# One attention loop in place of two, keys first in the context projection, and three experts over all tokens

## The chip, the cores and the metric

The kernel runs on one core of a Trainium2 chip. The metric is the device time of one execution in microseconds (us), the median of the runs. Everything is fp32 data; the large matrix products are made of three matmuls on `fp32r` halves (high by high, high by low, low by high), so that each weight tile is first split by ScalarE (ACT, `whi`) and VectorE (DVE, `wlo`) before TensorE (PE) uses it.

## The reference, cut to what matters

Two transformer blocks of two layers each over 256 tokens and 1024 channels. The change lies in layer two ("odd") of the first block: a projection, two attentions, an output projection, and a mixture of experts.

```python
p_lat = h_lat @ w_in                       # 256 x 2304: cq, dq, ck, cv, dk, dv
cq_l, dq_l = query_side(p_lat[..., :OD_Q], True)      # rms_norm by head, then rope
ck_l, cv_l, dk_l, dv_l = kv_side(p_lat[..., OD_Q:], True)
p_ctx = h_ctx @ w_in[:, OD_Q:]             # 256 x 1280: ck, cv, dk, dv of the context
ck_c, cv_c, dk_c, dv_c = kv_side(p_ctx, False)        # rms_norm and gain, no rope
y_lat = merge(window_gqa(cq_l, ck_l, cv_l, ck_c, cv_c, sink),      # 8 heads, sink in the sum
              diff_attention_latent(dq_l, dk_l, dv_l, dk_c, dv_c, lam))  # 4 heads, p0 - lam * p1
# merge: rms_norm over each difference head, concatenate, @ w_out

logits = xt @ router                       # 8 experts, the best 2 of each token
gates = ...                                # 256 x 8, zero where an expert was not chosen
out = sum over e of gates[:, e:e+1] * ((silu(xt @ w1[e]) * (xt @ w3[e])) @ w2[e])   # width 1408
```

## The kernel before, in words

**The weight stream.** SyncE (SP) loads weights in units of 512 rows by 512 columns (1 MB) into a ring of four buffers `raw`. ACT copies each half of a unit to `whi` (L326), DVE subtracts to `wlo` (L330), and PE runs the matmuls of L422, L423 and L426: 24 of them for a unit over both token tiles (`t` = 0, 1). `Split.step` on ACT and DVE splits the unit that comes two later; work between the halves of a step waits until PE has used the unit (`w_used`). A hook (`with_`) runs after each step with its number `i`: the small work of a stage is put there (`odd_q_*`, `odd_k_*`). Each engine runs its instructions in the order in which its function was written; semaphores join the engines. Nothing else decides the order.

**The projection of layer two.** `project_pe` makes the latent projection `pl` (blocks of 512 columns in the order of `OD_ORDER[0]`) and then the context projection `pc` (1280 columns: blocks of 512, 512 and 256). The first 128 columns of `pc` are the window keys, 128 are window values, then 512 difference keys and 512 difference values. During the context projection DVE finishes the latent keys: `odd_products_dve` and `odd_turn_dve` (rope, in hooks 1 and 2), `odd_scaled_dve` and `odd_twins_dve` with the root from GpSimd (POOL, `root_pool`), the lambda (hook 2), and then sums, gains and roots of the context keys (hooks 4 and 5). ACT waits in hook 4 for the sums `ss_c`. PE then transposes keys in `odd_k_pe` into `kTo`, first of all `out_done` and `k_lat`.

**The two attentions.** `attn_pe`, `attn_act` and `attn_dve` run a software pipeline over items: 16 window items (8 heads by 2 token tiles; scores of 512 keys and a mask matmul), then, as a second loop, 16 difference items. For item `i`, PE makes the scores of `i + 1`, transposes the probabilities of `i`, and makes the outputs of `i - 1`; DVE takes the maximum of the scores and copies the transposed probabilities of `i - 1` out of PSUM; ACT takes the exponential. Between the loops `heads_out_dve`, `heads_out_pe` and `heads_out_act` divide and transpose the window outputs. After the second loop `diff_out_dve` makes the difference, its squares and the root (POOL), scales, and PE transposes (`heads_out_pe(e, "att_d")`) between the two halves of the output projection `odd_out_pe`. All but the last of this chain lies on DVE alone.

**The experts.** `router_pe` and `router_dve` rank the logits, count the tokens of each expert and sort the experts by that count (`order`, `ids`); SP reads `ids` and loads the weights in that order. `wide(i)` is 2 for the first three experts of the order (256 slots) and 1 for the other five (128 slots). Tokens go into slots by a 0/1 matrix `sel`: `gather_pe` multiplies the rows of `x` (kept as `xmhi`, `xmlo`) by it, 16 matmuls a half, `select_pe` transposes it and picks the gates (`share`), and `scatter_pe` brings the outputs (`ohi`, `olo`) back to tokens. For the first three experts `added_dve` adds the scattered sum to `y`; from the fourth on the sums stay in PSUM.

## Time and profile before

| | |
|---|---|
| time, median of 3 runs | 2864.03 us (2858.02 to 2865.65) |
| the profiled execution: time / span | 2857.71 us / 2855.9 us |
| PE busy / weight loads | 2702.7 us (95%) / 2245.4 us |
| DVE, ACT, POOL busy | 1853.0 us (65%), 1466.5 us (51%), 164.1 us (6%) |
| chain that ended last, by engine | PE 84%, DVE 8%, ACT 3%, DMA 2%, issue 2% |
| HBM read | 507.33 MB, 178 GB/s over the span |

The profiled execution is 6.3 us under the median of the three runs. The chain is followed back from the last instruction: at each step to what released it, or to the instruction before it on its engine. A row of the timeline has its start, its length, the engine, the line of the kernel and, in brackets, how long the engine stood idle before it and what released it; consecutive instructions of one kind are merged, and their count follows the `x`. "PEclk" is TensorE's granted clock, with 1.00 for 2.4 GHz and 0.50 for 1.2 GHz.

### The profile page before, as it was taken

How to read it: one execution, taken by the hardware profiler on the slowest of the kernel's cores; microseconds unless marked ns; L12 is line 12 of the kernel's file. 1: busy time of each engine (PE TensorE's matmuls, PEld its weight loads, DVE VectorE, ACT ScalarE, POOL GpSimd, SP SyncE). 2: the span in 40 equal slices, each digit the busy share in tenths (PEclk: the TensorE clock that was granted, in tenths of full speed). 3: DMA queues.
4: the chain of work that ended last, by engine and by line, in shares of the span. 5: the costliest groups of instructions: out<-in, count | busy, mean ns of one | idle time of the engine just before them, and what ended most of it. 6: DMA issues, size and time to landing. Idle time of an engine off the chain costs nothing.

```text
span 2855.9 us, 34338 instructions
## 1 busy us (share of the span) xinstructions
PE 2702.7 (95%) x13129; PEld 2245.4 (79%) x13129; DVE 1853.0 (65%) x2344; ACT 1466.5 (51%) x2095; POOL 164.1 (6%) x206
## 2 busy tenths in 40 slices
PE   7998899999989889999999899998799999998998
PEld 5776678888875678888888788877678788787787
DVE  6676687787694555556878655588556555546555
ACT  6563454444462244445777545664355544563553
POOL 2111000000120000000000000002010000100100
PEclk9999999999998989999999999999899999999999
DMA  8672176776740045546999656540255555550444
GB/s 297 231 255 88 66 244 229 241 274 209 228 156 1 1 163 184 171 162 213 332 322 320 234 162 206 163 162 1 82 183 182 182 189 175 200 192 16 143 159 147
DMA packets 260641, 511.43 MB, mean 179 GB/s; under 512 B 9641, under 2 KB 40577, under 8 KB 260368
## 3 DMA queue, kind: packets, MB, share of 16 engines
q1 hardware_dynamic: 256576, 498.11, 51.7%
q0 software_dynamic: 3920, 11.36, 1.4%
q8 instruction: 95, 1.56, 0.2%
q14 instruction: 50, 0.41, 0.0%
HBM read 507.33 MB, written 1.05 MB: 178 GB/s over the span
## 4 chain that ended last, share of the span: by engine, by line
PE 84%; DVE 8%; ACT 3%; DMA 2%; issue 2%; POOL 0%; SPq 0%; DVEq 0%; ACTq 0%; POOLq 0%
PE bank L422 23%; PE bank L423 22%; PE bank L426 22%; PE bank L1378 2%; PE bank L1391 2%; DVE wlo L330 2%; DVE h_hid L2643 1%; PE bank L1404 1%; DMA raw<-in_moe_w 1%; PE bank L393 1%; PE bank L394 1%; PE bank L395 1%; ACT whi L326 1%; PE bank L2189 1%; PE bank L518 1%
## 5 line engine op out<-in xcount | busy, mean ns | idle before, releaser
L330 DVE TENSOR_TENSOR wlo<-raw,whi 128x1024 fp32r<-128x1024 f32 (+1 forms) x964 | 1140.8, 1199 | 693.8 <-ACT whi L326 687.8
L326 ACT ACTIVATE whi<-raw 128x1024 fp32r<-128x1024 f32 (+1 forms) x964 | 990.4, 1039 | 795.6 <-PE bank L426 757.7
L422 PE MATMUL bank<-whi,xhi 128*128 128x512 f32 (+2 forms) x2328 | 887.0, 381 | 20.1 <-DVE wlo L330 7.7
L426 PE MATMUL bank<-whi,xlo 128*128 128x512 f32 (+2 forms) x2328 | 878.2, 377 | 0.0
L423 PE MATMUL bank<-wlo,xhi 128*128 128x512 f32 (+2 forms) x2328 | 877.2, 377 | 0.0
L422 PEld LDWEIGHTS bank<-whi,xhi 128*128 128x128 f32 x2328 | 441.4, 190 | 102.1 <-issue 16.1
L426 PEld LDWEIGHTS bank<-whi,xlo 128*128 128x128 f32 x2328 | 440.5, 189 | 77.4
L423 PEld LDWEIGHTS bank<-wlo,xhi 128*128 128x128 f32 x2328 | 441.5, 190 | 74.6
L422 PE MATMUL bank<-whi,f_hhi 128*128 128x512 f32 x496 | 194.1, 391 | 0.0
L426 PE MATMUL bank<-whi,f_hlo 128*128 128x512 f32 x496 | 193.1, 389 | 0.0
L423 PE MATMUL bank<-wlo,f_hhi 128*128 128x512 f32 x496 | 193.1, 389 | 0.0
L1446 ACT ACTIVATE tmp<-bank,negm 128x512 f32<-128x512 f32 (+2 forms) x112 | 60.8, 543 | 145.9 <-DVE negm L1430 111.5
L426 PEld LDWEIGHTS bank<-whi,f_hlo 128*128 128x128 f32 x496 | 93.1, 188 | 19.4
L423 PEld LDWEIGHTS bank<-wlo,f_hhi 128*128 128x128 f32 x496 | 93.2, 188 | 19.0
L422 PEld LDWEIGHTS bank<-whi,f_hhi 128*128 128x128 f32 x496 | 93.1, 188 | 18.9
L422 PE MATMUL bank<-whi,m_hhi 128*128 128x512 f32 x242 | 96.1, 397 | 0.9 <-DVE wlo L330 0.8
L426 PE MATMUL bank<-whi,m_hlo 128*128 128x512 f32 x242 | 94.6, 391 | 0.0
L423 PE MATMUL bank<-wlo,m_hhi 128*128 128x512 f32 x242 | 94.4, 390 | 0.0
L618 DVE TENSOR_TENSOR f_hlo<-bank,f_hhi 128x512 fp32r<-128x512 f32 (+1 forms) x66 | 42.8, 687 | 71.9 <-ACT f_hhi L574 71.7
L1430 DVE TENSOR_REDUCE negm<-bank 128x1 f32<-128x256 f32 (+2 forms) x96 | 45.8, 479 | 59.1 <-PE bank L1380 31.3
L574 ACT ACTIVATE f_hhi<-bank 128x512 fp32r<-128x512 f32 (+1 forms) x66 | 36.2, 595 | 82.6 <-PE bank L518 82.6
L1404 PE MATMUL bank<-kb,tmp 128*128 128x128 f32 x296 | 57.3, 297 | 14.9 <-ACT tmp L1446 13.2
(546 smaller groups left out, 2890.7 us busy)
## 6 DMA issues: line engine op xcount, KB each, us to landing
raw<-in_ffn_w SPq DMA_DIRECT2D x180, 1024.0 KB, 5.1
raw<-in_moe_w SPq DMA_DIRECT2D x96, 1024.0 KB, 5.7
raw<-in_moe_w SPq DMA_DIRECT2D x48, 768.0 KB, 4.7
raw<-in_ada_w SPq DMA_DIRECT2D x24, 1024.0 KB, 5.3
raw<-in_ev_w_in SPq DMA_DIRECT2D x24, 1024.0 KB, 5.8
raw<-in_ffn_w SPq DMA_DIRECT2D x36, 512.0 KB, 3.5
raw<-in_hyb_w_in SPq DMA_DIRECT2D x18, 1024.0 KB, 5.0
raw<-in_attn_w_qkv SPq DMA_DIRECT2D x18, 1024.0 KB, 5.1
```

The source lines that it names most:

```text
L326: nc.scalar.activation(whole, part, ACT.Copy).then_inc(sem("w_hi"), 1)
L330: nc.vector.tensor_tensor(wlo[s][:, 0:rows, 0:n], part, whole.bitcast(F32), ALU.subtract)\
L422: nc.tensor.matmul(bank[:, 0:n], xk_h, whi[s][:, wk, 0:n], start=first, stop=False)
L423: ins = nc.tensor.matmul(bank[:, 0:n], xk_h, wlo[s][:, wk, 0:n], start=False, stop=last and xl is None)
L426: ins = nc.tensor.matmul(bank[:, 0:n], xk_l, whi[s][:, wk, 0:n], start=False, stop=last)
L574: ins = nc.scalar.activation(hhi[:, at, :].rearrange("p k t -> p (k t)"), T[b // TOK][:, 0:k * TOK], ACT.Copy)
L618: ins = nc.vector.tensor_tensor(hlo[:, at, :].rearrange(flat), T[b // TOK][:, 0:k * TOK], hhi[:, at, :].bitcast(F32).rearrange(flat), ALU. ...
L1378: nc_last = nc.tensor.matmul(bank[:, 0:n], it["q"], it["k"], start=True, stop=not adds)
L1391: ins = nc.tensor.matmul(it["o"], probT[i % 2][:, k * P:k * P + P], it["v"][k], start=k == 0, stop=k == kt - 1)
L1404: ins = nc.tensor.transpose(PT[i % 2][:, k * P:k * P + P], prob[i % 2][:, k * P:k * P + P], ident)
L1430: nc.vector.tensor_reduce(col, SC[i % 2][:, 0:it["n"]], AX.X, ALU.max, negate=True)\
L1446: nc.scalar.activation(prob[i % 2][:, 0:it["n"]], SC[i % 2][:, 0:it["n"]], ACT.Exp, bias=negm[:, i:i + 1], accum_out=den[:, i:i + 1]).then ...
```

## The change

Three edits, all in layer two of the first block:

1. **Keys.** `OD_ORDER[1]` makes the context blocks 512, 256 and 512 columns, so that all keys come before the difference values, and `narrow_units` splits only 256 columns of a narrow unit. The rope of the latent keys and the gains of the context keys move from DVE to POOL (`odd_keys_pool`, `odd_gain_pool`). The latent difference keys are transposed inside the last block (`odd_lat_pe`, ahead of its second unit), the rest after it.
2. **Attention.** One loop over 32 items. The window outputs are divided, transposed and cut inside it (`odd_every_dve`, `odd_aside_pe`, `odd_also_act`), and so is the first half (two heads) of the difference. The second half follows the loop (`diff_out_dve`), and each half has its own transposes, inside the first two units of the output projection (`diff_turn_pe`).
3. **Experts.** The first three experts of the order (`DENSE = 3`) run over all 256 tokens, with the gate column `weight` in the product in place of `share`, and DVE adds their outputs to `y` directly. They have no `select`, `gather` or `scatter`. `x` is cut on DVE ahead of `router_dve` (`moe_c`), and `xmlo` is made after the first four weight halves are split (`rows_dve`).

```diff
-    OD_ORDER = ([c * N for c in (0, 1, 4, 2, 3)], None)
+    OD_ORDER = ([c * N for c in (0, 1, 4, 2, 3)], [(0, N), (N, N // 2), (N + N // 2, N)])
...
+    def odd_keys_pool(e):
+        quad = lambda ap: ap.rearrange("p (h a b c) -> p h a b c", a=2, b=2, c=16)
+        e.after("sq_k1")
+        for t in range(NT):
+            for hd, n, g in K_PARTS:
+                part, at = pl[:, t, hd * HD:(hd + n) * HD], hd % 16 * HD
+                cos = gcos[:, t, g, :].rearrange("p (o d) -> p o d", o=1).broadcast_to([P, n, HD])
+                e.put(nc.gpsimd.tensor_tensor(by_head(cos_part[:, at:at + n * HD]), by_head(part), cos, ALU.mult))
...
+    def odd_lat_pe(e):
+        e.after("k_lat", "qoT1")
+        for b in range(4):
+            for t in range(NT):
+                at, c = 1280 + b * P, b % 2 * TOK + t * P
+                ins = nc.tensor.transpose(T[b // 2][:, c:c + P], pl[:, t, at:at + P], ident)
+        e.put(ins, "dlT_ps")
...
-        if i in (1, 2):
-            odd_products_dve(e, i - 1, K_PARTS)
-            for hd, n, _ in K_PARTS:
-                odd_turn_dve(e, i - 1, hd, n)
...
         if i == 3:
-            e.after("k_o:root")
+            e.after("k_o:root", "k_turned1")
...
+    W_END, W_TURNS, D_HALF = 16, (20, 22), 24
+    def odd_every_dve(e, base):
+        def every(i):
+            if i == W_END:
+                window_sinks_dve(e, base)
+            if i == W_END + 1:
+                window_out_dve(e, base)
+            if i in (25, 28):
+                cut_x(e, "cat_o", (i // 28,), lambda b: f"att_w:oT{b}")
+            if i in (26, 27):
+                if i == 26:
+                    diff_shares_dve(e, base, 0)
+                diff_scale_dve(e, 0, i - 26)
+            if i == 29:
+                diff_add_dve(e, 0)
+            if i in (30, 31):
+                diff_squares_dve(e, 0, i - 30)
+        return every
...
+    def diff_out_dve(e, s, base):
+        diff_finish_dve(e, 0)
+        diff_shares_dve(e, base, 1)
+        for t in range(NT):
+            diff_scale_dve(e, 1, t)
+        diff_add_dve(e, 1)
+        for t in range(NT):
+            diff_squares_dve(e, 1, t)
+        s.step()
+        diff_finish_dve(e, 1)
+        cut_x(e, "cat_o", (2,), lambda b: f"att_d:oT{b}")
+        s.step()
+        cut_x(e, "cat_o", (3,), lambda b: f"att_d:oT{b}")
...
+        items[0]["o_free"] = lambda e: e.after("att_w:o")
...
+    DENSE = 3
...
             for j, n in enumerate(widths(FE)):
                 e.eng.wait_ge(sem("silu_done"), f.pairs.at(0))
-                if j == 0:
-                    e.after(f"moe_x{i}1", *(["moe_xlo01"] if i == 0 else []))
+                if j == 0 and i >= DENSE:
+                    e.after(f"moe_x{i}1")
                 s.unit(xhi, xlo, 0, 4, n, G[:w], True, False)
-                if j == 0:
-                    if i:
-                        e.eng.wait_ge(sem("y_done"), f.ys.at(0))
-                        scatter_pe(e, i - 1)
-                    else:
-                        select_pe(e, 0)
...
+                if j == 0 and i > DENSE:
+                    e.eng.wait_ge(sem("y_done"), f.ys.at(0))
+                    scatter_pe(e, i - 1)
...
                 odd_k_out(e)
-                attn_act(e, ATT0[2], W_ITEMS)
-                window_sinks_act(e)
-                heads_out_act(e, "att_w", 0)
-                attn_act(e, ATT0[3], D_ITEMS)
+                attn_act(e, ATT0[2], W_ITEMS + D_ITEMS, lambda i: odd_also_act(e, i))
...
             if on(4):
                 moe_norm_dve(e)
+                cut_x(e, "moe_c", range(4), lambda b: f"moe:xf{2 * b + 1}")
                 router_dve(e)
```

What the edits do to the order on three engines follows. First POOL, from the root of the queries (`ss` of 32 columns) to the root of the difference heads. Before:

```order
L795 TENSOR_SCALAR ss<-ss 128x32
L796 TENSOR_TENSOR ss<-ss,mhalf 128x32
L795 TENSOR_SCALAR ss<-ss 128x24
L796 TENSOR_TENSOR ss<-ss,mhalf 128x24
L795 TENSOR_SCALAR ss<-ss 128x8
```

And of the change, the same place (`o_kT` holds the two products for the time being, `o_pl` is the latent projection; the eight instructions from L1851 to L1860 come a second time, for the other token tile, ahead of the row that follows here):

```order
L801 TENSOR_TENSOR ss<-ss,mhalf 128x32
L1851 TENSOR_TENSOR o_kT<-o_pl,o_gcos 128x128
L1854 TENSOR_TENSOR o_kT<-o_pl,o_gsin 128x4x16 x2
L1851 TENSOR_TENSOR o_kT<-o_pl,o_gcos 128x512
L1854 TENSOR_TENSOR o_kT<-o_pl,o_gsin 128x16x16 x2
L1860 TENSOR_TENSOR o_pl<-o_kT 128x128
L1860 TENSOR_TENSOR o_pl<-o_kT 128x512
```

Sixteen instructions stand between the root of the queries and that of the keys (24 columns), and four more (L1871, the gains) behind it.

Second, PE where the context projection ends and the attention begins (`o_sq` holds the doubled window keys, `o_pl` and `o_pc` the difference keys; the L1378 or L1383 matmul is the first score). Before:

```order
L1959 MATMUL bank<-kb,o_sq 128x128 [waits dve_done,out_done]
L1959 MATMUL bank<-kb,o_sq 128x128 x3
L1963 MATMUL bank<-kb,o_pl 128x128 x8
L1967 MATMUL bank<-kb,o_sq 128x128 [waits dve_done]
L1967 MATMUL bank<-kb,o_sq 128x128 x3
L1974 MATMUL bank<-kb,o_pc 128x128 [waits dve_done]
L1974 MATMUL bank<-kb,o_pc 128x128 x7
L1378 MATMUL bank<-o_kT,o_qT 128x512 [waits act_done,dve_done]
```

Of the change, first between the two units of the last block, then behind that block:

```order
L426 MATMUL bank<-whi,xlo 128x512
L1995 MATMUL bank<-kb,o_pl 128x128 [waits act_done,dve_done,w_lo]
L1995 MATMUL bank<-kb,o_pl 128x128 x7
L422 MATMUL bank<-whi,xhi 128x512
L423 MATMUL bank<-wlo,xhi 128x512
```

```order
L2013 MATMUL bank<-kb,o_sq 128x128 [waits dve_done,out_done]
L2013 MATMUL bank<-kb,o_sq 128x128 x7
L2019 MATMUL bank<-kb,o_pc 128x128 [waits dve_done]
L2019 MATMUL bank<-kb,o_pc 128x128 x7
L1383 MATMUL bank<-o_kT,o_qT 128x512 [waits act_done,dve_done,out_done]
```

The eight transposes of the latent difference keys now stand ahead of 24 matmuls of the projection, with a wait on DVE (`k_lat`) and on ACT (`qoT1`).

Third, PE from the last count of the router to the first expert's first matmuls. Before:

```order
L2082 MATMUL bank<-m_mask,ones 128x8
L2189 MATMUL bank<-m_sel,m_xmhi 128x256 [waits dve_done]
L2189 MATMUL bank<-m_sel,m_xmhi 128x256 x7
L2189 MATMUL bank<-m_sel,m_xmlo 128x256 x8
L2189 MATMUL bank<-m_sel,m_xmhi 128x256 x8
L2189 MATMUL bank<-m_sel,m_xmlo 128x256 x8
L422 MATMUL bank<-whi,xhi 128x512 [waits dve_done,w_lo,act_done,silu_done]
```

Of the change:

```order
L2246 MATMUL bank<-m_mask,ones 128x8
L2247 MATMUL bank<-m_mask,ones 128x8
L422 MATMUL bank<-whi,xhi 128x512 [waits dve_done,w_lo,silu_done]
L423 MATMUL bank<-wlo,xhi 128x512
L426 MATMUL bank<-whi,xlo 128x512
```

The gather and its wait are gone; what the first expert waits for is the cut `x` and its weights.

## Rows read from the trace of the kernel before

**Rows 1.** Engines by stretch: us, busy of PE, PEld, DVE, ACT, POOL, PEclk, DMA share, GB/s

```profile
817.00:858.00 41.00, 32.76 (x173) 27.76 (x171) 37.46 (x60) 24.30 (x34) 4.41 (x2) 0.88 0.35 116
1024.00:1029.30 5.30, 5.25 (x12) 4.13 (x13) 3.31 (x3) 1.49 (x2) 0.00 (x0) 0.50 0.50 171
1131.00:1233.00 102.00, 102.00 (x506) 88.33 (x506) 53.31 (x59) 47.85 (x65) 0.00 (x0) 1.00 0.54 171
1391.00:1601.00 210.00, 204.34 (x1010) 174.95 (x1009) 174.59 (x180) 156.91 (x192) 0.00 (x0) 0.99 0.95 328
```

**Rows 2.** PE's waits from 817 to 992 us, the longest: total, times, longest

```profile
PE bank L1959 <- ACT o_pc L755: 6.3, 1, 6.3
```

**Rows 3.** Timeline of PE from the context projection to the output projection

```profile
825.03 1.03 PE L1951 MATMUL bank<-kb,o_pl 128*128 128x128 f32 x8
...
851.46 1.91 PE L1963 MATMUL bank<-kb,o_pl 128*128 128x128 f32 x8
...
858.77 2.04 PE L1378 MATMUL bank<-o_kT,o_qT 64*128 64x512 f32 x2 [1.00 <-DVE o_kT L1989]
...
869.40 1.12 PE L1378 MATMUL bank<-o_kT,o_qT 64*128 64x512 f32 x2
...
901.81 1.12 PE L1378 MATMUL bank<-o_kT,o_qT 64*128 64x512 f32 x2
...
925.71 1.12 PE L1378 MATMUL bank<-o_kT,o_qT 64*128 64x512 f32 x2
...
958.28 0.61 PE L1391 MATMUL bank<-o_pc,tmp 128*128 128x128 f32 x4
...
970.74 1.09 PE L1715 MATMUL bank<-kb,tmp 128*128 128x128 f32 x8 [0.92 <-DVE tmp L2035]
...
986.91 1.88 PE L1069 MATMUL bank<-gates,ones 128*128 128x512 f32 x4
```

**Rows 4.** Timeline of ACT: the squares of the latent keys

```profile
820.75 1.56 ACT L1886 ACTIVATE o_sq<-o_pl 128x768 f32<-128x768 f32 x2
```

**Rows 5.** Timeline of DVE between the two attention loops and inside the second

```profile
908.02 1.80 DVE L1706 TENSOR_TENSOR tmp<-bank,den 128x256 f32<-128x256 f32 x4
...
926.87 0.69 DVE L1430 TENSOR_REDUCE negm<-bank 128x1 f32<-128x512 f32 x1 [1.25 <-PE bank L1378]
```

**Rows 6.** Timeline of POOL and DVE where the rope tables are made

```profile
784.89 0.74 POOL L1800 TENSOR_TENSOR o_gcos<-o_gain,o_rope 128x256 f32<-128x256 f32 x1
...
786.47 1.33 DVE L330 TENSOR_TENSOR wlo<-raw,whi 128x1024 fp32r<-128x1024 f32 x1 [2.40 <-ACT whi L326]
786.80 1.60 POOL L1800 TENSOR_TENSOR o_gcos<-o_gain,o_rope 128x256 f32<-128x256 f32 x1
```

**Rows 7.** POOL's instructions by form: count, busy us, mean ns, idle before

```profile
L2761 POOL TENSOR_TENSOR tmp<-kb,cols 128x512 f32<-128x512 f32 x4 | 14.8, 3736 | 135.5 <-PE bank L2587 135.5
...
L796 POOL TENSOR_TENSOR ss<-ss,mhalf 128x24 f32<-128x24 f32 x1 | 4.2, 4173 | 0.1
...
L2761 POOL TENSOR_TENSOR hc<-kb,cols 128x512 f32<-128x512 f32 x2 | 2.1, 1094 | 0.0
```

**Rows 8.** Timeline of DVE and PE from the sorted expert ids on

```profile
1009.60 0.17 DVE L2118 CAST m_ids<-m_kept 128x8 int32<-128x8 f32 x1
...
1014.38 2.04 PE L2189 MATMUL bank<-m_sel,m_xmhi 128*128 128x256 f32 x8 [7.15 <-DVE vtop L2131]
...
1022.68 4.63 DVE L330 TENSOR_TENSOR wlo<-raw,whi 128x1024 fp32r<-128x1024 f32 x4 [0.77 <-ACT whi L326]
...
1024.06 0.77 PE L422 MATMUL bank<-whi,xhi 128*128 128x512 f32 x1 [3.47 <-DVE wlo L330]
```

**Rows 9.** The page's DMA issues: count, KB each, median us to landing

```profile
raw<-in_moe_w SPq DMA_DIRECT2D x96, 1024.0 KB, 5.7
```

**Rows 10.** The chain that ended last, inside the wide experts: start, us, what

```profile
1107.17 1.91 PE bank L2189 x16
...
1131.45 3.63 PE bank L2236 x16
```

More of the change, by code:

```diff
@@ L1901, in odd_k_act @@
                       f"qoT{i // 4}")
+        if i == 5:
+            e.after("dlT_ps")
+            for b in range(2):
+                e.put(nc.scalar.activation(kTo[:, 2 + 2 * b:4 + 2 * b, 0:TOK], halves(T[b][:, :]), ACT.Copy), "dlT")
         if i == 4:
@@ L1986, in odd_k_take @@
     def odd_k_take(e):
-        for b in (1, 2, 3):
-            e.after(f"dkT_ps{b}")
-            e.put(nc.vector.tensor_copy(kTo[:, 2 + b, :], psum[2 + b][:, :]), "dkT")
+        twins, diffs = key_banks(e)
+        e.after("dkT_ps")
+        for b in range(2):
+            e.put(nc.vector.tensor_copy(kTo[:, 2 + 2 * b:4 + 2 * b, TOK:2 * TOK], halves(diffs[b][:, :])), "dkT")
     def lambda_dve(e):
@@ new lines, in diff_turn_pe, with diff_turn_act @@
+    def diff_turn_pe(e, half):
+        e.after(f"att_d:o{half}")
+        for k in range(2):
+            for t in range(NT):
+                c = k * TOK + t * P
+                ins = nc.tensor.transpose(psum[4 + half][:, c:c + P], diff_head(half, t)[:, k * P:k * P + P], ident)
+        e.put(ins, f"att_d:oT_ps{half}")
+    def diff_turn_act(e, half):
+        e.after(f"att_d:oT_ps{half}", "sublng")
+        e.put(nc.scalar.activation(xf[:, 4 + 2 * half:6 + 2 * half, :].rearrange("p k t -> p (k t)"), psum[4 + half][:, :],
+                                   ACT.Identity, scale=sublng[:, 0:1]), f"att_d:oT{2 + half}")
@@ L2192, in gather_pe @@
         e.put(ins, f"moe_ps{i}{r}")
-    def first_gather_act(e):
-        for r, banks in enumerate(FIRST_BANKS):
-            e.after(f"moe_ps0{r}")
-            for j in range(2):
-                k0 = 4 * r + 2 * j
-                e.put(nc.scalar.activation(xhi[:, k0:k0 + 2, :], banks[j][:, :].rearrange("p (k t) -> p k t", k=2),
-                                           ACT.Copy), f"moe_x0{r}")
     def gather_act(e, i, r):
```

306 lines of the change are left out of this document (176 added, 130 removed).

## The prediction

> **What bounds the kernel now.** I read the stretches of the span first. In the wide experts TensorE is busy for the whole of 102 us at the full granted clock [rows 1], so there an instruction taken off PE is time taken off the end. In the narrow experts (1391 to 1601) PE is still 97% busy, but the DMA share is 0.95: two bounds side by side. In the context projection (817 to 858) DVE is busy 37.46 of 41 us and PE only 32.76, and PE's longest wait in the region is 6.3 us, for the last projection block, which ACT could not take out of PSUM because it stood in its hook waiting for DVE's sums [rows 2]. So the stage is DVE's. Then I read PE's timeline through the attention [rows 3]: it starts at 858.77, its pitch between 869.40 and 901.81 is 32.41 / 12 = 2.70 us an item and PE has no gap there, so the loop is PE's; between the two loops, and between the halves of the output projection (from 969.8 on, 0.92 us of idle and then transposes), PE stands or runs light.
>
> **The sum** is of four terms: the keys, the joined loop, the tail behind it, and the experts.
>
> **1. Keys (costs 6 us).** DVE loses its rope and gains, which is what made it late. But PE now waits for `k_lat` in the middle of the projection, and `k_lat` waits for POOL. When does POOL finish? It starts when the squares of the latent keys are done, at 820.75 + 1.56 = 822.3 [rows 4]. It has two times eight instructions: one product of 512 columns, two of 256, one sum of 512, and four of 128 or 64. Alone, 256 columns took 0.74 us [rows 6] and 512 took 1.09 [rows 7]. With about 0.4 for each small one that is 1.1 + 1.5 + 1.1 + 1.6 and eight gaps of 0.08 (an estimate) = 5.8 a tile, 11.6 us for both. They won't run alone. The second table product began at 786.80 while DVE was in a weight split (786.47 to 787.80) and took 1.60 in place of 0.74: the 0.86 more is what was left of the split [rows 6]. I charge POOL the DVE instructions with two SBUF inputs that fall into this stretch: the second half of the query scaling, four wide and two narrow splits, lambda's small ones, about 8.8 us (1.2 for each wide one, by 1.33 and by 4.63 / 4 [rows 6, 8]). So the keys are turned at 822.3 + 11.6 + 8.8 = 842.7. The root of 24 columns takes 4.17 [rows 7] and its scale 0.3: 847.3. DVE's scaling of the keys, some 2.4 us, and a little contention with POOL's gains give `k_lat` at about 850.3.
>
> The Trainium skill ("SBUF — State Buffer", "Who interferes with whom") has the pair of ports shared by DVE and GpSimd as an exclusive lock, held for a whole instruction, which a DVE instruction with two SBUF inputs contends for. The 1.60 agrees; by that rule alone the charge would be what I took. It speaks against this edit: what DVE gives up comes back as waits on both.
>
> PE meanwhile: block one ends at 825.03 [rows 3], eight transposes 1.03, two narrow units of half of 5.46 each, eight transposes, one unit: 825.0 + 1.0 + 5.5 + 1.0 + 5.5 = 838. (A unit of 24 matmuls took 5.46: between the outputs' end, 958.89, and 970.74 - 0.92 = 969.82 lie two [rows 3].) So PE stands from 838 to 850. Even with a free POOL it would stand until 842, since `qoT1` comes behind ACT's weight copy, two squares (1.56) and two copies of 1.1 together [rows 4]. After a stop that long the clock is low: the same eight transposes took 1.91 at 851.46 against 1.03 at 825.03 [rows 3], and the first expert's 12 matmuls took 5.25 us at a granted 0.50 [rows 1]. So: transposes 1.9, the unit 5.25 + 2.73 = 8.0, then ACT's take, weight copy, latent keys and window keys at 1.1 each and gaps, 4.6. The attention starts at 850.3 + 14.5 = 864.8 against 858.77: 6.0 us late. The two sides: POOL without contention gives `k_lat` at 822.3 + 11.6 + 4.5 + 2.4 = 840.8, so PE's resumption at 842.1 by `qoT1`, a start at 856.6, 2 us early; POOL slowed as in its worst row (3736 against 1094 ns, a factor of 3.4, beside a DVE busy without pause [rows 7]) gives 822.3 + 39.4 + 4.5 + 2.4 = 868.6 and a start 24 us late. I take the middle one: DVE is busy here with gaps, as at 786.80, not without.
>
> The start of the loop is at the low clock in both kernels (10.6 us from 858.77 to the fourth score at 869.40), so it cancels.
>
> **2. Joined loop (saves 8.3).** Before, five score intervals, from 901.81 (the last window item) to 925.71 (the fifth difference item), took 23.9 us [rows 3], since the loop drained, the window outputs were divided and transposed, and the new loop filled at the low clock. Joined they take 5 x 2.70 = 13.5 (an upper bound; difference items lack the mask matmul): 10.4 saved. The eight window transposes are now inside, 1.0. In item 17 DVE divides the window outputs (1.80 [rows 5] and about 0.6 before it) while PE's outputs of item 16 wait for that bank (`o_free`): the division ends 4.0 us after the scores of 17, PE is there after 3.1, so 0.9 stall, and 0.2 for the two waits on ACT's turned window heads. The other insertions are 0.9 to 1.9 us in items in which DVE stood idle for 1.25 us [rows 5] and PE, which makes the next scores first, has about 1.0 of slack behind it (an estimate): no cost. Twelve such insertions without that cover would cost some 12 us together. 10.4 - 1.0 - 0.9 - 0.2 = 8.3.
>
> **3. Tail (saves 4.7).** From the loop's end (958.28 + 0.61) to the end of the fourth unit (986.91) it took 28.0 us [rows 3]: two units 10.9, then DVE's chain late (0.92), transposes 1.09, and 15.1 for the copies, the cut and two units, partly at the low clock. Now half the difference is ready in the loop; DVE's other half (shares, four scalings, two sums, four squares, POOL's root) takes 5.7 us, then two weight halves until 8.2 and the finish until 9.1, under two units and four transposes that last until 11.5. Then four transposes, a wait of 0.3 for the last cut, and two units: 11.5 + 0.6 + 0.3 + 10.9 = 23.3. 28.0 - 23.3 = 4.7. If the cover fails, the finish is what is late next.
>
> **4. Experts (saves 27.4).** Scatters of the first three experts are gone: 16 matmuls, 3.63 us each [rows 10], 10.9. Gathers of the second and third: two of 1.91 each [rows 10], 7.6. Three `select` of eight light matmuls, as long as eight transposes, 1.1 [rows 3] each, with their entries 3.6. DVE's four adds (about 2.5 us) that made the fourth expert's weights late, 0.8. All of it stood on a PE that never waits [rows 1]. What replaces it, four DVE additions into `y` per expert, lies where four subtractions lay, with DVE half idle. The start: the ids were ready at 1009.77 [rows 8]; the cut of `x`, ahead of the router, makes them about 1.0 later (its last pair follows ACT's last `xf`). A weight unit lands 5.7 us after its issue [rows 9], issued 1.0 after the ids: 1010.8 + 1.0 + 5.7 = 1017.5, less 0.5 because the queue is empty; ACT's copy (about 1.1) and DVE's 1.2 put the first matmul at 1019.5 in place of 1024.06 [rows 8]: 4.5 saved. The low clock of its first 5.3 us stays [rows 1]. Sum 10.9 + 7.6 + 3.6 + 0.8 + 4.5 = 27.4.
>
> **Sum:** -6.0 + 8.3 + 4.7 + 27.4 = 34.4 us off the profiled 2857.71, so 2823.3. The median of the three runs lies 6.3 above the profiled execution; I carry that over: 2864.0 - 34.4 = 2829.6, and give **2829.5 us**.
>
> **Rivals.**
> *A. The keys cost nothing.* POOL and DVE share peacefully, or the splits fall into POOL's gaps. For it: POOL is idle but for 4.41 of the 41 us [rows 1]. Against: the 1.60. The keys then give +2: total 42.4, 2821.6.
> *B. POOL as slow as in its worst row.* For it: the 3736 ns. Against: there DVE had no gaps. The keys cost 24: total 16.4, 2847.6.
> *C. The narrow experts are the DMA's.* With share 0.95 [rows 1], PE comes earlier but the weights don't; the last scatter (3.6) and the 0.8 are not gained, nor is all that DVE did for the ring. Total 30, 2834. Against: 97% PE busy there, and the ring is full whenever a wide expert ends.
> *D. Slower than before.* Again POOL's keys, with everything behind them: PE stands inside the projection from 838 on for as long as it takes. It decides against the change once the attention starts 40.4 us late, the worth of the other three terms: `k_lat` at 858.8 + 40.4 - 14.5 = 884.7, each POOL instruction some 5 times its price alone. No row shows more than 3.4 times.
> *E. The edits do less than they say*: an insertion in the loop that stalls PE each time, or a change in the dense experts that brings a wait of DVE on PE for every bank. Terms 2 and 3 gone: total 21, 2843.
>
> **Chances.** Forecast 0.52, A 0.17, B 0.09, C 0.12, D 0.02, E 0.08. A measurement of this kernel tells about 0.3% (8.6 us) from no change. All but D are faster by more than that, and even B only if no other goes wrong with it: faster 0.94, same 0.04, slower 0.02. The range runs from A, with 4 us for the runs' own spread, to between C and E: 2817 to 2843.
>
> **What would show it.** Term 1: PE idle in front of the L1995 transposes, released by DVE `o_pl`, from about 838 to 850, POOL's L1851 to L1860 spread over 20 us, and the first L1383 score at 865; right if 862 to 868, rival A if under 858. Term 2: 32 scores with no gap over 1 us, the end of the outputs 86 to 90 us after the first score. Term 3: 23 to 24 us from there to the gates' matmuls. Term 4: the first expert matmul 4 to 5 us nearer to the router's, wide experts 5 to 9 us shorter each, no L2189-like rows before the third expert's end, and the first narrow expert without a DVE wait. The prediction is wrong if the narrow experts lengthen by what the wide ones gave, if PE's clock stays low in the joined loop, or if the wait in the projection is not POOL's.

## The result, and the profile after

| | before | after |
|---|---|---|
| median of the runs | 2861.03 us (4 runs, 2856.73 to 2865.65) | 2815.07 us (4 runs, 2812.31 to 2817.93) |
| the profiled execution: time / span | 2857.71 / 2855.9 us | 2817.79 / 2816.0 us |
| mean granted clock of that execution | 0.969 | 0.971 |

The ratio is 0.984 (95% interval 0.9822 to 0.9859), which is 46 us off. I had forecast 34.4 off and 2829.5; the measured median lies 2 us under my range. The terms of the forecast can be read one by one: I cut the traces at the same places and subtract. Before's places are in [rows 3, 8], and its last scatter stands at 1597.18; the other columns come from the same instructions of the changed kernel in three profiled executions ("again" and "third" are the first two runs of the next section). The "qoT0 transposes" are the first eight query transposes behind a projection block, a "score" is the start of the score matmuls of one attention item, and the "gates' matmuls" (L1069 before, L1074 after) are the first of PE behind the output projection. "Saved" compares the before and after columns alone.

| stretch | before | after | again | third | saved | forecast |
|---|---|---|---|---|---|---|
| start of the qoT0 transposes, from the span's start | 825.03 | 828.32 | 825.98 | 823.58 | | |
| 1: from there to the fourth score | 44.37 | 44.84 | 44.91 | 44.93 | -0.5 | -6.0 |
| 2: to the end of the last outputs | 89.49 | 80.43 | 80.28 | 80.89 | 9.1 | 8.3 |
| 3: to the gates' matmuls | 28.02 | 23.25 | 23.24 | 23.22 | 4.8 | 4.7 |
| 4a: to the first expert matmul | 37.15 | 32.67 | 32.54 | 36.14 | 4.5 | 4.5 |
| 4b: to the last scatter | 573.12 | 547.66 | 547.17 | 548.21 | 25.5 | 22.9 |

The savings come to 43.3 in all (before rounding), against 34.4. What stands between 43.3 and the 39.9 of the two profiled executions are the 3.3 us by which the changed one came late to the stage, where nothing was edited.

First the stretches of the changed kernel that answer to [rows 1] (the same columns), and PE's longest waits from 820 to 995 us, which answer to [rows 2]:

```profile
820.00:861.00 41.00, 31.04 (x174) 26.94 (x172) 30.67 (x37) 21.21 (x33) 25.23 (x22) 0.92 0.39 129
1009.51:1014.81 5.30, 5.30 (x15) 4.24 (x16) 5.11 (x7) 2.39 (x3) 0.00 (x0) 0.63 1.05 387
1102.00:1204.00 102.00, 102.00 (x486) 87.57 (x485) 55.83 (x59) 45.30 (x52) 0.00 (x0) 1.00 0.59 187
1351.00:1561.00 210.00, 205.41 (x1014) 175.75 (x1013) 174.52 (x181) 157.56 (x192) 0.00 (x0) 0.99 0.96 330
```

```profile
PE bank L1995 <- DVE o_pl L1881: 8.8, 1, 8.8
PE bank L869 <- DVE tmp L2226: 6.5, 1, 6.5
PE bank L1383 <- DVE o_kT L2037: 2.9, 1, 2.9
PE bank L1396 <- DVE hc L2075: 0.6, 1, 0.6
```

The wait that I named is there, on `k_lat`, and is longer (8.8) than the 6.3 of [rows 2]. DVE's load in the stage fell from 37.5 to 30.7 of 41 us and POOL's rose from 4.4 to 25.2. PE's timeline, as [rows 3] for before:

```profile
828.32 1.04 PE L1986 MATMUL bank<-kb,o_pl 128*128 128x128 f32 x8
...
850.24 1.94 PE L1995 MATMUL bank<-kb,o_pl 128*128 128x128 f32 x8 [8.79 <-DVE o_pl L1881]
857.92 1.03 PE L2013 MATMUL bank<-kb,o_sq 128*128 128x128 f32 x8
858.79 1.04 PE L2019 MATMUL bank<-kb,o_pc 128*128 128x128 f32 x8
862.75 1.52 PE L1383 MATMUL bank<-o_kT,o_qT 64*128 64x512 f32 x2 [2.92 <-DVE o_kT L2037]
...
873.16 1.29 PE L1383 MATMUL bank<-o_kT,o_qT 64*128 64x512 f32 x2
...
913.49 1.12 PE L1383 MATMUL bank<-o_kT,o_qT 64*128 64x512 f32 x2
915.82 0.68 PE L1396 MATMUL bank<-o_pl,tmp 128*128 128x128 f32 x4 [0.62 <-DVE hc L2075]
...
952.98 0.61 PE L1396 MATMUL bank<-o_pc,tmp 128*128 128x128 f32 x4
...
968.55 0.47 PE L422 MATMUL bank<-whi,xhi 128*128 128x512 f32 x1 [0.37 <-DVE xlo L1314]
976.84 1.88 PE L1074 MATMUL bank<-gates,ones 128*128 128x512 f32 x4
```

POOL's keys in the timeline, the new work that [rows 6, 7] had to stand for:

```profile
825.32 0.57 POOL L1851 TENSOR_TENSOR o_kT<-o_pl,o_gcos 128x128 f32<-128x128 f32 x1 [14.94 <-ACT o_sq L1927]
825.85 2.03 POOL L1854 TENSOR_TENSOR o_kT<-o_pl,o_gsin 128x64 f32<-128x64 f32 x2
...
839.43 2.56 POOL L1860 TENSOR_TENSOR o_pl<-o_kT 128x128 f32<-128x128 f32 x2
842.08 0.21 POOL L800 TENSOR_SCALAR ss<-ss 128x24 f32<-128x24 f32 x1
842.37 4.18 POOL L801 TENSOR_TENSOR ss<-ss,mhalf 128x24 f32<-128x24 f32 x1
846.63 4.63 POOL L1871 TENSOR_TENSOR o_pc<-o_pc,o_gain 128x128 f32<-128x128 f32 x4
```

The rope lasts from 825.32 to 841.99, 16.7 us, where I had put 20.4; the root is as long as in [rows 7], and DVE stands 6.16 us for the end of the rope and the root. `k_lat` ends at 850.13, 21.8 after the qoT0 transposes; I had 850.3 - 825.0 = 25.3.

### The profile page after: what moved, and what is told of

It is laid out like the page before. It is cut to its first block, busy times and chain, and to the rows that moved or that the text cites. A ratio compares the mean times of both kernels' runs of the same rounds, so it can differ in the third digit from the quotient of the medians.

```text
span 2816.0 us, 33938 instructions
## 1 busy us (share of the span) xinstructions
PE 2667.4 (95%) x12949; PEld 2218.3 (79%) x12949; DVE 1839.1 (65%) x2323; ACT 1445.0 (51%) x2052; POOL 183.8 (7%) x228
## 4 chain that ended last, share of the span: by engine, by line
PE 86%; DVE 6%; ACT 3%; DMA 2%; issue 2%; POOL 1%; SPq 0%; DVEq 0%; ACTq 0%; POOLq 0%
PE bank L422 23%; PE bank L423 23%; PE bank L426 23%; PE bank L1383 2%; PE bank L1396 2%; DVE h_hid L2788 1%; PE bank L1411 1%; PE bank L393 1%; PE bank L394 1%; PE bank L395 1%; ACT whi L326 1%; PE bank L518 1%; DMA raw<-in_moe_w 1%; DVE wlo L330 1%; PE bank L1385 1%
## 5 line engine op out<-in xcount | busy, mean ns | idle before, releaser
L422 PE MATMUL bank<-whi,xhi 128*128 128x512 f32 (+2 forms) x2328 | 889.7, 382 | 24.9 <-issue 12.8
```

The source lines that it names most:

```text
L422: nc.tensor.matmul(bank[:, 0:n], xk_h, whi[s][:, wk, 0:n], start=first, stop=False)
```

## The experiments

In all of them the stretches of the table are the measure, read from one profiled execution each; the median of four to twelve runs stands beside. A stretch can be read to a tenth, but the clock moves it from one execution to the next, and how far is part of what follows.

**The changed kernel again, and a third time.** No edit.

> The changed kernel itself, unchanged, a second time. Two things are to be read. First, which numbers repeat: from the eight qoT0 transposes to the first score of the attention 34.4 us, first score to the end of the last outputs 90.8, from there to the gates' matmuls 23.3, to the first expert matmul 32.7, first expert matmul to the last scatter 547.7; each should come within 0.3. Second, the 3.3 us by which the changed kernel's profiled execution reached the projection of layer two late, with no edit ahead of it. Theory: this is the clock that TensorE was granted in stops of the first 400 us (mean 0.91 against 0.96 from 100 to 140 us, 0.96 against 1.00 from 270 to 310), which differs from execution to execution; then executions of this one kernel fall at both about 2812.3 and 2817.9, the shorter with the higher mean clock (0.974 to 0.975 against 0.971). Rival: the program's new order or code size delays its early stages; then the qoT0 transposes stand at 828.3 again, whatever the mean clock.

> The changed kernel on the same chip as the version above, to compare the two directly. Its median should be 2814 to 2816 as on the two occasions before, its executions between 2812 and 2822, the shorter with the higher mean clock. The keys' stretch, qoT0 transposes to fourth score, again 44.9 within 0.2 (theory: set by POOL's and DVE's chain and two stops), or else 43 or 41 (rival: it hangs on the clock too).

Medians 2814.81 (2813.39 to 2821.79) and 2818.83 (2817.50 to 2821.16), ratios to the kernel before 0.9834 (0.982 to 0.9848) and 0.9849 (0.9833 to 0.9864). The third median lies above the 2814 to 2816 that I expected, so medians of one kernel, taken at different times and on different chips, differ by 4 us. The stretches repeat as the table shows, but for 4a in the third (36.14). Stretch 1 repeats only as a sum: the start of the attention and the way from there to the fourth score trade (34.43 + 10.41, 35.77 + 9.14, 34.95 + 9.98).

The first part of it can be followed in these three traces and in the five others below that have the same keys' code. PE resumes at 21.9 us, by `k_lat`, in all eight. The unit behind it takes 5.7 to 7.1 us, by the clock. The first score starts 4.83 us behind that unit's end in all eight: ACT takes the block out of PSUM, copies the last weight half and the keys, and DVE's second split waits for that weight copy. In "again":

```profile
857.12 1.09 ACT L759 ACTIVATE o_pc<-bank 128x512 f32<-128x512 f32 x2 [1.60 <-PE bank L426]
859.18 1.22 DVE L330 TENSOR_TENSOR wlo<-raw,whi 128x1024 fp32r<-128x1024 f32 x1 [1.81 <-ACT whi L326]
```

So PE's chain sets the start in this kernel, and DVE's ends 0.5 to 1.8 us ahead of it (what DVE idles there, 0.47 to 1.85 us). How long the scores behind the start stay slow is a second draw. In five of the eight traces the item behind the fourth score takes 2.7 to 3.3 us. In the three others (edit 1 alone, the 36 matmuls and those ahead of the router) it takes 5.0 to 5.1, and stretch 1 does not count it: in the latter two it makes stretch 2 82.8 and 82.7.

The arrival at the stage doesn't repeat, and the stretches of the early stages say why. From 100 to 140 us in before, after and the third:

```profile
100.00:140.00 40.00, 38.05 (x175) 31.05 (x174) 23.00 (x22) 18.61 (x24) 0.00 (x0) 0.96 0.61 204
```

```profile
100.00:140.00 40.00, 38.05 (x168) 30.94 (x167) 21.57 (x21) 18.51 (x23) 0.00 (x0) 0.91 0.60 193
```

```profile
100.00:140.00 40.00, 38.05 (x182) 31.26 (x181) 23.49 (x22) 19.79 (x26) 0.00 (x0) 1.00 0.66 219
```

The same busy time, and a clock of 0.96, 0.91 and 1.00. Summed over the first 820 us in steps of 10, one less the granted clock comes to 15.4, 20.4, 17.2 and 15.3 us in the four profiles of the table. The rival, that the new order delays the early stages by a fixed amount, is out: the third stood at the transposes at 823.58, ahead of before's 825.03. (All fourteen traces of edited kernels arrive between 823.58 and 829.70.) But the higher clock isn't always the shorter run, as I had expected: the third arrives first and then loses it again in stretch 4a (36.14).

**Edit 1 alone.** The kernel before with the keys' edit; two loops, tail and experts as before.

> The kernel before with edit 1 alone: blocks of 512, 256, 512, rope and gains on POOL, the latent difference keys transposed inside the last block; two attention loops, tail and experts as before. My forecast of the term was a cost of 6.0 us; the two traces give 0.7 (34.43 against 33.74 from the qoT0 transposes to the first score). Theory by the traces: start at 34.4, the total 0 to 1.5 above the kernel before. Forecast as written: start at 40, total 6 above it. Rival: the keys' edit helps the loop behind it (ordering, clock), total below the kernel before by more than 1.

2862.90 us (12 runs), ratio 0.9999 (0.9988 to 1.0009). Stretch 1 is 35.06 + 9.87 = 44.93, 0.6 above before's. Stretch 2 is 91.63 against 89.49, for the slow fourth interval (5.03 us in place of 2.70). So the keys cost 0.5 to 0.6 us to the fourth score, 2.7 with the stretch behind it in this trace, in which the clock came back late (whether the keys' edit makes that likelier isn't shown), and nothing that can be told in the time. My 6.0 are refuted; there is no gain either.

**Edit 3 alone, and edits 1 and 2 alone.**

> The kernel before with edit 3 alone (the three widest experts over all tokens, the cut of x ahead of the router). The stretch from the gates' matmuls to the last scatter is 610.3 us before and 580.3 to 579.7 in the changed kernel's two profiles. Theory: the parts are independent, so this kernel has 580 there, 30 us less than before (my forecast had 27.4: 10.9 scatters, 7.6 gathers, 3.6 selects, 0.8 wait, 4.5 start), and its time is 29 to 31 below the kernel before's. Forecast as written: 27 to 28 below. Rival: part of the 30 hangs on the other edits (what state the clock is in when the router begins, or the weights already in the ring), and this kernel gets 25 or less.

> The kernel before with edits 1 and 2 (keys, one attention loop, its tail), experts as before. Theory by the traces: keys cost 0.5 to 0.7, the loop saves 9.3, the tail 4.8: 13.5 below the kernel before; first score to the end of the outputs 90, then 23.2 to the gates. Forecast as written: 8.3 + 4.7 - 6.0 = 7.0 below. Rival: the edits help each other, so that this one and the experts' alone add up to less than the changed kernel's 46 to 47; by the first theory they add up to 43 to 46.

Edit 3 alone: 2828.43 us, ratio 0.9888 (0.9871 to 0.9904), which is 32 off (27.5 to 36.9); stretches 4a and 4b are 32.30 and 547.01. Edits 1 and 2: 2851.47, ratio 0.9959 (0.9944 to 0.9973), 12 off (8 to 16); stretches 1 to 3 are 44.89, 80.43, 23.23. Together 44 by the medians, with 4 to 5 us either way on each, and each stretch is that of the changed kernel to 0.7 us: no dependence between the parts can be seen. Edit 2 has no run of its own; its share is what edits 1 and 2 save beyond edit 1. In its router and experts this profile stands 2.6 us above before's (37.76 and 575.15), with waits of PE on DVE's `tmp` of 1.2 and 2.4 us that before's had not.

**The latent keys' transposes last.** Taken out of the last block, put behind the other key transposes; ACT's copies of them move too.

```diff
-                            if i == 1:
-                                s.needs[4] = lambda: odd_lat_pe(e)
...
         e.put(ins, "dkT_ps")
+        odd_lat_pe(e)
```

> The changed kernel with the transposes of the latent difference keys moved from inside the last projection block to behind all other key transposes, so that PE does not wait for k_lat between its two last units (8.8 us idle there, and the unit behind it at a low clock at first). Theory P, my prediction's working (attention start = k_lat + transposes + unit + copies): the unit runs in the gap, ends at about 847, and the attention starts 4 to 5 us earlier, 30 after the qoT0 transposes in place of 34.4; the total is 4 to 5 us less than the changed kernel's. Theory D, from the changed kernel's trace: the chain to the start is DVE's (k_lat at 850.1, two splits 3.3, the sums 1.9, ACT's root, reciprocal, twins 0.9, scaling 1.4, k_ctx at 858.4, two more splits and the copies), and it does not hear of PE's stop: start at 33 to 35, total within 1.5 us of the changed kernel's.

2818.70 us (2812.04 to 2821.57). PE no longer stands inside the projection, and yet the first score comes at 34.10 (34.43 to 35.77 above) and the fourth at 43.71, 1.2 less. That is Theory D's number. Now PE waits for the window keys from DVE:

```profile
853.27 1.94 PE L2009 MATMUL bank<-kb,o_sq 128*128 128x128 f32 x8 [10.24 <-DVE o_sq L1887]
```

DVE has no gap there but 0.44 us for a root on ACT from `k_lat` on (two splits, sums, root, twins), so its chain sets the start here. In the changed kernel it did not, against Theory D: there it ended just ahead of PE's. And the transposes, 5.3 us for all 24 after PE's longer stop and at the low clock, took back part of what was gained. The median is no lower than the changed kernel's (2814.81 in runs taken at the same time); in the profiled execution stretch 4a is 36.57. The 10 us around the router's matmuls, in the changed kernel first and in this one:

```profile
984.00:994.00 10.00, 8.77 (x56) 8.65 (x57) 6.52 (x15) 4.84 (x10) 1.06 (x3) 0.67 0.00 1
```

```profile
984.00:994.00 10.00, 10.00 (x49) 9.90 (x48) 6.93 (x21) 3.76 (x8) 0.00 (x0) 0.50 0.00 1
```

The clock was 0.50 throughout, and the 32 router matmuls took 6.83 in place of 4.06 us. The third run of the changed kernel, with no edit, has 6.84 too, so this is not the edit's doing.

**Rope back on DVE.** Its hooks as before, `odd_keys_pool` gone, gains still on POOL.

```diff
+        if i in (1, 2):
+            odd_products_dve(e, i - 1, K_PARTS)
+            for hd, n, _ in K_PARTS:
+                odd_turn_dve(e, i - 1, hd, n)
         if i == 2:
             lambda_dve(e)
         if i == 3:
-            e.after("k_o:root", "k_turned1")
+            e.after("k_o:root")
```

> The changed kernel with the rope of the latent keys back on DVE, in the hooks where it was; the gains stay on POOL. Theory D: DVE spends 6.3 us more (two times 3.15), but in the changed kernel it stood 6.16 us for POOL's root behind POOL's rope; now the root runs beside DVE's rope, and uncontended splits take 1.2 each again. k_lat comes 1 to 2 us earlier, at 20 to 21 us after the qoT0 transposes in place of 21.8, the start of the attention 1 to 2 us earlier, 32.5 to 33.5, and the total is 1 to 2 us less. Rival: the offload is what made the keys cheap (0.7 in place of the 6.0 that I forecast); then without it DVE is 4 to 6 us late, start at 38 to 40, total 4 to 6 more.

2813.35 us (2810.22 to 2814.84), ratio 0.982 (0.9808 to 0.9833). Stretch 1: 32.56 + 9.05 = 41.61, 3.3 less than with the rope on POOL. PE resumes at 18.9 in place of 21.9, 3.0 earlier and more than my 1 to 2, and its wait for `k_lat` is halved:

```profile
844.86 1.94 PE L1999 MATMUL bank<-kb,o_pl 128*128 128x128 f32 x8 [4.40 <-DVE o_pl L1881]
```

So the offload was no gain but a loss inside edit 1. 3.0 us of it are firm, in `k_lat`; the 3.3 at the fourth score are of one trace and hang on the clock too. DVE had the time, since it stood waiting for the root, which now runs on POOL beside DVE's rope. In the time it does not show by itself: the changed kernel's runs of the same time have a median of 2814.81, 1.5 more, and the two sets overlap.

**Both: rope on DVE, transposes last.**

> The changed kernel with both: rope of the latent keys on DVE (it brought the fourth score, counted from the qoT0 transposes, from 44.9 to 41.6 us) and the latent difference keys' transposes last (44.9 to 43.7). If both gains are in the same chain, DVE's, they add only in part: fourth score at 40 to 41.5, total 3 to 5 below the changed kernel's. If PE's stop for k_lat, 4.4 us in the rope kernel, is what still sets the start, the fourth score comes at 37 to 38.5 and the total 6 to 8 below.

2812.82 us (2806.54 to 2817.68), the profiled execution 2806.54. Stretch 1: 31.99 + 6.55 = 38.54, 6.4 less than the changed kernel's. That is the second expectation's number, but not by its reason: the first score comes only 0.6 us earlier than with the rope alone on DVE, and the other 2.5 are the clock, which in this execution was back by the first score (6.54 from the first to the fourth, in place of 9.05). DVE and POOL in this kernel:

```profile
841.62 4.97 POOL L1871 TENSOR_TENSOR o_pc<-o_pc,o_gain 128x128 f32<-128x128 f32 x4 [8.14 <-ACT o_sq L1936]
...
843.27 4.40 DVE L330 TENSOR_TENSOR wlo<-raw,whi 128x1024 fp32r<-128x1024 f32 x2
```

**Gains back on DVE too.** From that kernel; the four products stand ahead of the reciprocal.

```diff
-                odd_gain_pool(e)
...
-            e.after("std_c", "gain_c")
+            for hd, n, g in ((0, 2, 2), (4, 8, 3)):
+                for t in range(NT):
+                    part = by_head(pc[:, t, hd * HD:(hd + n) * HD])
...
+            e.after("std_c")
```

> The kernel with rope on DVE and the latent difference keys last, and now the gains of the context keys back on DVE too, so that POOL has nothing but the root of the keys. In its parent POOL's four gain products took 4.97 us from 841.62, and two DVE splits beside them took 4.40 in place of 2.36, a second scaling 0.83 in place of 0.69. Theory, contention: what the offload takes off DVE (2.07 us) it gives back in DVE's slower instructions (2.04 + 0.14); so without it the splits take 2.36 again, and the fourth score stays within 0.5 us of the parent's 38.5 after the qoT0 transposes. Rival: the offload does take work off DVE's chain, and the fourth score comes 1.5 to 2.1 us later.

2811.80 us (2809.44 to 2815.07), ratio 0.9819 (0.9801 to 0.9837).

```profile
844.63 2.36 DVE L330 TENSOR_TENSOR wlo<-raw,whi 128x1024 fp32r<-128x1024 f32 x2
...
848.88 2.07 DVE L1976 TENSOR_TENSOR o_pc<-o_pc,o_gain 128x128 f32<-128x128 f32 x4
```

The two splits are back at 2.36 us and the gains take 2.07: what POOL took off DVE it took back, 2.04 of 2.07. The first score comes at 31.28 in place of 31.99. The fourth comes at 40.96, 2.4 later than in the parent, and by its number alone the rival would hold. But the last version below has the same keys and 31.29 + 6.54 = 37.83, so the 3.1 between the two are the clock's. The first 10 us of the attention in this kernel, then in the last version:

```profile
857.47:867.47 10.00, 9.23 (x27) 5.33 (x27) 3.91 (x8) 4.91 (x10) 0.00 (x0) 0.66 0.00 0
```

```profile
860.97:870.97 10.00, 9.52 (x42) 5.28 (x42) 5.30 (x11) 5.21 (x12) 0.00 (x0) 1.00 0.00 0
```

**PE kept busy ahead of the experts,** by 36 and then by 54 matmuls into a bank that is overwritten.

```diff
         follow(e, s, "moe_c")
+        e.after("moe_c:x3")
+        for _ in range(36):
+            nc.tensor.matmul(G[1][:, :], xhi[:, 0, 0:P], xhi[:, 0:2, :].rearrange("p k t -> p (k t)"),
+                             start=True, stop=True)
```

> The changed kernel with 36 matmuls of 512 columns put on PE, into a PSUM bank whose content is then overwritten, between the router's last count and the first expert's first matmul, where PE stood 11.8 us for weights. They change nothing that is computed. Theory: the granted clock was 0.67 over the first 6 us of the experts because PE had stood; kept busy, PE has the full clock there, and the first 31 us of the first expert shorten by 2 to 2.6 us, the total too, if the 36 end before the weights land (7.8 us at full clock, 15.5 at half: between 1005.5 and 1013). Rival: at half clock they last until 1013 and delay the first expert by up to 3.5; total 0 to 2 more. Rival two: activity doesn't matter and the clock is low as before; no change.

> The changed kernel with 54 matmuls in place of 36 ahead of the experts. With 36 they took 8.41 us, PE then stood 3.66 us, and the first matmuls of the expert ran at the low clock all the same (0.77 and 0.63 us for the first rows of one), so that the experts took 548.7 in place of 547.4. Theory: even 3.7 us of standing are enough to lose the clock; 54 take 12.6 us and end within 0.5 us of the moment at which the weights land (11.8 to 12.1 after the last count), the expert starts at the full clock and the stretch from first expert matmul to last scatter is 2.0 to 2.8 shorter, 544.8 to 545.6, against a start up to 0.5 later. Rival: the first expert's slow matmuls come from something else, its weights or its split; then 547 to 548.7 again.

With 36 the 3.66 us that were left sufficed to lose the clock. The end of them and the first expert:

```profile
1000.32 8.41 PE L2410 MATMUL bank<-xhi 128*128 128x512 f32 x36
1012.40 0.77 PE L422 MATMUL bank<-whi,xhi 128*128 128x512 f32 x1 [3.66 <-issue]
```

With 54 there is no gap, and the first matmul runs at full clock:

```profile
995.27 12.55 PE L2410 MATMUL bank<-xhi 128*128 128x512 f32 x54
1007.65 0.39 PE L422 MATMUL bank<-whi,xhi 128*128 128x512 f32 x1
```

The first expert, first matmul to the next one's, takes 92.65 in place of 94.60 us: 2.0 for the low clock, as expected. But stretch 4b is 546.94, not 545: the narrow experts and the wait for the last outputs took 264.6 from the fourth expert's start, in place of 263.4. Medians 2823.31 (four runs, 2813.32 to 2824.31) and 2818.12 (2814.83 to 2828.07): no gain in the time could be told.

**PE kept busy ahead of the router,** 24 such matmuls into `O[0]` before the transposes of the normed tokens.

> The changed kernel with 24 matmuls of 512 columns, whose result is not used, where PE stands 6.5 us before the transposes of the normed tokens ahead of the router. Those 16 transposes took 3.68 us and the 32 router matmuls 4.06 at a clock of 0.5 to 0.84; in the kernel with the latent keys last the same 32 took 6.83, all at 0.50, and the stretch from the gates' matmuls to the first expert was 36.6 in place of 32.7. Theory: the stretch hangs on the instant at which the full clock comes back; with 5.6 us of the 6.5 filled it is full throughout, transposes 2.1, router matmuls 3.4 or less, stretch 30 to 31.5, total 1 to 2.5 less. Rival: 0.9 us of standing in light work loses it anyway, stretch 32.7 or 36.6 as before.

2818.82 us (2815.97 to 2824.32). The 16 transposes took 2.2 (two times 1.09) in place of 3.68, but the router matmuls 3.81 and PE then waited: 32.00 for stretch 4a, 0.5 to 0.7 better than the changed kernel's good draws, and stretch 4b 550.9. The 1 to 2.5 us were not there. The narrow experts took 266.7 here, but 266.6 in the kernel with the gains on DVE too, which has no added matmuls; the cause was not tried.

**The last version:** rope and gains on DVE, transposes last, 54 matmuls ahead of the experts; on one chip with the third run of the changed kernel.

> The changed kernel with rope and gains back on DVE, the latent difference keys' transposes last, and the 54 matmuls that keep PE busy ahead of the experts. From the profiles: the fourth score 3.9 to 6.3 us earlier (41.0 or 38.5 after the qoT0 transposes, against 44.9), the first expert 1.9 shorter, its start 0.3 to 0.5 later. If all of it reaches the end, the median is 5.5 to 8 below that of the changed kernel on the same chip. Rival: the first part does, but the narrow experts give the second back in waits for DVE and weights (263.1 to 264.6 from the fourth expert's start to the last scatter with the 54): 3 to 5 below. Rival two: what the clock gives in one place it takes in another, and the median is within 2 of the changed kernel's.

2812.80 us (2810.26 to 2814.14, five runs) against 2818.83 (2817.50 to 2821.16, four runs): 6.0 us faster than the changed kernel in runs taken at the same time, within the 5.5 to 8 of the expectation, and no run of the one reaches the other. Against the changed kernel's two earlier medians, 2815.07 and 2814.81, it would be 2. Ratio to the kernel before 0.9823 (0.981 to 0.9837). Stretch 1 is 37.83 against 44.93. Its profile arrived at 829.68 against 823.58 and still ended 3.5 us sooner (2814.04 against 2817.50). So what the keys' stretch gains, 3.9 us in the one profile with this code and 7.1 in the other, reaches the end at least in part; how much of the 6.0 is that, how much the 54 matmuls and how much the spread of such medians can't be told from this pair.

## Why the prediction was off

The mechanisms were all there; two sizes were wrong where it matters: term 1 cost 0.5 us where I had charged 6.0, and term 4 gave 29.9 where I had 27.4. The sizes were 8.9 us short in the sum of the terms; the rest of the 11.6 between 34.4 and 46.0 is which executions the medians hold (before's came down from 2864.0 to 2861.0 with its fourth run, against 2857.71 profiled; the changed kernel's lies 2.7 under its profiled one). The range was too narrow on that side: its low end was rival A, in which term 1 alone changes, and left no room for terms 2 and 4 to be larger as well.

**Term 1 failed, by 5.5 us.** Two steps of it. "I charge POOL the DVE instructions with two SBUF inputs that fall into this stretch ... about 8.8 us": the rope took 16.7 us, which with my 11.6 for it alone makes 5.1, and brought `k_lat` 3.5 us sooner than forecast. The small instructions suffered (128 x 64 took 1.17 us mean where I had put 0.4), the 512-column ones hardly (1.29 against 1.09). The Trainium skill ("SBUF — State Buffer", "Who interferes with whom") has the shared pair of ports as an exclusive lock, for which a DVE instruction with two SBUF inputs contends with GpSimd's reads; that the pair is held for a whole instruction it says of DVE's two-port modes. The traces agree in kind, with DVE's two splits at 4.40 against 2.36 beside the gains, but charging POOL each DVE instruction in full was 3.7 us too much. And "After a stop that long the clock is low ... the unit 5.25 + 2.73 = 8.0": from the end of the transposes (852.18) to the next ones at 857.92 the unit took 5.7, in the other profiles up to 7.1. The clock was back sooner than in the first expert, whose 12 slow matmuls I had carried over. The path was the right one: `k_lat`, transposes, unit, and 4.83 us to the first score where I had 4.6. What it lacks is that DVE's path was nearly as long, so that taking PE's stop away gained only 1.2. And the start of the loop does not cancel, as I had put it, in any one pair of traces: the way from the first to the fourth score took 6.5 to 10.6 us in the fifteen profiles. That this came out near zero against before (10.4 against 10.6) is luck of the execution.

That the offload was the dangerous part was right in sign: with the rope on DVE `k_lat` came 3.0 us sooner and stretch 1 was 3.3 us shorter. The rest of edit 1 paid for it, so that the sum came to 0.5. Rival A (POOL's sharing costs nothing) had the total nearly right and the reason wrong.

**Term 2 was mis-sized, by 0.8** (0.3 and 0.9 by the two other profiles). I took five intervals at 2.70 as an "upper bound" and left it there; the difference items run at 2.53, so five take 2.70 + 4 x 2.53 = 12.8, not 13.5. The stall by `o_free` is 0.86 (0.9 forecast), the two transposes in the loop 0.43 each (1.2 forecast with their waits), the other insertions nothing. Of the 9 saved, about 6 was the low clock between the loops (an estimate: PE's instructions from 909.87 to 925.71 took 15.8 us, and with the lengths that the same kinds have at full clock, and the one wait of 1.38, they come to 9.9). From 908 to 923 us before, and in the changed kernel:

```profile
908.00:923.00 15.00, 11.73 (x31) 6.66 (x32) 5.15 (x9) 3.53 (x8) 0.00 (x0) 0.57 0.00 0
```

```profile
908.00:923.00 15.00, 14.38 (x78) 8.90 (x76) 9.25 (x19) 4.78 (x13) 0.00 (x0) 1.00 0.00 1
```

31 instructions in one and 78 in the other, at 0.57 and 1.00.

**Term 3 was right:** 4.8 against 4.7 (4.8 in all three profiles), with the wait of 0.37 where I had 0.3.

**Term 4 was mis-sized, by 2.5.** The start came out at 4.5, in part by luck: the ids came 0.5 us later where I had 1.0, the first matmul 9.3 behind them where I had 8.7, and in the third profile only 1.0 was left of it, for the slow router matmuls. Inside, from the first matmul of one expert to that of the next (before, after): 101.78, 94.60; 101.44, 92.61; 100.64, 97.01; 56.24, 51.36. The third pair differs by exactly one scatter, 3.63 (3 x 3.63 = 10.9 as forecast). The second pair has 5.20 more than a scatter: two gathers are 3.82 of it, as forecast, and the `select` 1.37, not 1.1 to 1.2. The first pair has no scatter, but two gathers and two `select`, 6.6, and 0.6 for a clock that came back sooner (0.63 against 0.50 in its first 5.3 us). The fourth expert gave 1.25 besides the scatter, where I had 0.8, and the narrow ones 0.9 together, where rival C had them give back 4.4. In these two profiles the narrow ones do not give back what the wide ones gave, although the DMA share is 0.96; rival C's loss is not there.

Left open: from the fourth expert's start to the last scatter it takes 263.0 to 266.7 us in the twelve profiles with the dense experts, with waits of PE on DVE's `tmp` that differ (0.8 us in the changed kernel, 3.1 in the one with the gains on DVE too). No run was made on that, and it is as large as most of the gains above.

## What to carry to other kernels

Before work is moved to POOL to relieve DVE, look at what DVE would wait for there: with a root on POOL behind the moved work, DVE stood 6.2 us for 5.8 us of relief (its two ropes in the rope kernel, 2.96 and 2.88), and an instruction moved beside DVE's splits cost DVE as much as it had saved (2.04 of 2.07). Follow the chain behind a long wait to its end before pricing the wait: 8.8 us of a standing PE were worth 1.2, since DVE's chain ended only 0.5 to 1.8 us sooner. And price the end of a pipelined loop by its clock as well as its drain: joining two loops gave 9 us, of which about 6 was clock. And don't judge a change of 1 to 3 us by one trace: the same code reached the fourth score at 37.8 and at 41.0.

## What the runs showed of the hardware

The clock after a stop does not come back after a fixed time. The same 32 router matmuls of the same kernel took 4.06 us in one execution and 6.84 in another, and the same early stage ran at 0.91, 0.96 and 1.00; the differences from execution to execution are a few us at each place, and they are of the size of the spread of one kernel, 2812 to 2822 us. The Trainium skill ("TensorE: Matmul & The Clock Gate", "Part 1: The HAM clock gate (the "warmup" mystery)") says that the number of slow matmuls at a kernel's start differs from run to run of one kernel; the traces agree, and show it inside a kernel too, with the 4.06 and 6.84 us. After 8.4 us of dense matmuls a standstill of 3.7 us was enough, in the one trace that has it, for the next matmul to run at half the clock (0.77 us). Filling a standstill with matmuls whose result is not used does raise the clock behind it (0.39 us for the first matmul in place of 0.77), and returned 2.0 us there, but nothing that could be told at the end of the kernel.
